# Attention steps over both key heads in halves of the TensorE array, with turning and values inside a later main tile

## What is computed

```python
s = jnp.einsum('bnqhgd,bnjhd->bnhgqj', qb, kb) * (HEAD_DIM ** -0.5)
s = jnp.where(valid, s, NEG_INF)
sk = sink.reshape(N_KV_HEADS, GQA_GROUP)
m = jnp.maximum(jnp.max(s, axis=-1, keepdims=True), sk)
e = jnp.exp(s - m)
p = e / (jnp.sum(e, axis=-1, keepdims=True) + jnp.exp(sk - m))
o = jnp.einsum('bnhgqj,bnjhd->bnqhgd', p, vb)
```

## Time and profile before

| | before |
|---|---|
| median of 3 runs | 1231.93 us |
| runs from, to | 1230.93, 1232.09 us |
| the profiled execution | 1237.62 us |
| its span | 1235.9 us |
| TensorE / VectorE / ScalarE / GpSimd busy | 97% / 56% / 30% / 6% |
| TensorE in the chain that ended last | 88% |

### The profile page before, as it was taken

How to read it: one execution, slowest core, us unless ns; L and a number is a source line. 1 busy time by engine, 2 the same in 40 slices (tenths; PEclk the granted TensorE clock), 3 DMA queues, 4 the chain that set the end, 5 groups by cost and what they waited for, 6 DMA issues and landing times.

```text
span 1235.9 us, 17238 instructions
## 1 busy us (share of the span) xinstructions
PE 1195.6 (97%) x6524; PEld 1090.1 (88%) x6524; DVE 691.9 (56%) x1146; ACT 365.1 (30%) x550; POOL 74.9 (6%) x104
## 2 busy tenths in 40 slices
PE   6979999999999999999999999999999999999997
PEld 1576668888899999999979999999999999999886
DVE  3777786887535575445645677653365333233434
ACT  3541114443451111232133532113311231123324
POOL 1100110000111111000000000000000000000000
PEclk7989999999999999999999999999999999999998
DMA  8833454231133232246421244332233221221212
GB/s 296 326 111 102 142 184 168 86 103 62 42 120 116 94 112 94 94 153 230 134 93 61 86 136 145 127 119 68 68 112 109 68 68 51 68 68 65 72 34 102
DMA packets 42528, 138.67 MB, mean 112 GB/s; under 512 B 4539, under 2 KB 10251, under 8 KB 41452
## 3 DMA queue, kind: packets, MB, share of 16 engines
q1 hardware_dynamic: 26832, 83.19, 20.0%
q0 software_dynamic: 10592, 41.95, 9.8%
q10 hardware_dynamic: 5052, 12.81, 3.0%
HBM read 122.20 MB, written 15.74 MB: 112 GB/s over the span
## 4 chain that ended last, share of the span: by engine, by line
PE 88%; DVE 7%; DMA 2%; issue 2%; ACT 1%; SPq 0%; DVEq 0%; ACTq 0%
PE acc_ps L561 61%; PE acc_ps L631 10%; PE wk L852 3%; PE wk L678 2%; PE wk L772 2%; PE wk L792 2%; PE wk L830 2%; DMA mod_raw<-in_w_ada_rows 1%; PE wk L782 1%; PE wk L671 1%; PE acc_ps L638 1%; DVE hy_cross L1605 1%; DVE dot_out L1404 1%; PE wk L592 1%; DMA hy_spec<-spec 1%
## 5 line engine op out<-in xcount | busy, mean ns | idle before, releaser
L561 PE MATMUL acc_ps<-act_hilo,w_hi 128*128 128x384 f32 x2304 | 510.2, 342 | 7.2 <-DVE act_hilo L1357 3.8
L561 PEld LDWEIGHTS acc_ps<-act_hilo,w_hi 128*128 128x128 f32 x2304 | 410.4, 189 | 29.1 <-issue 23.7
L561 PE MATMUL acc_ps<-act_hilo,w_lo 128*128 128x384 f32 x1152 | 294.2, 336 | 0.0
L1311 DVE TENSOR_TENSOR w_lo<-w_raw,w_hi 128x1024 fp32r<-128x1024 f32 x102 | 124.8, 1223 | 173.5 <-ACT w_hi L1001 172.5
L561 PEld LDWEIGHTS acc_ps<-act_hilo,w_lo 128*128 128x128 f32 x1152 | 209.8, 189 | 0.0
L1001 ACT ACTIVATE w_hi<-w_raw 128x1024 fp32r<-128x1024 f32 x102 | 108.0, 1059 | 286.8 <-PE acc_ps L561 283.2
L561 PE MATMUL acc_ps<-hidden_hilo,w_hi 128*128 128x384 f32 x768 | 164.0, 334 | 0.0
L561 PEld LDWEIGHTS acc_ps<-hidden_hilo,w_hi 128*128 128x128 f32 x768 | 135.9, 188 | 0.0
L561 PE MATMUL acc_ps<-hidden_hilo,w_lo 128*128 128x384 f32 x384 | 97.3, 334 | 0.0
L1715 DVE SCALAR_TENSOR_TENSOR xT<-acc_ps,modT,xT 128x384 f32 (+2 forms) x72 | 30.4, 479 | 89.8 <-PE acc_ps L561 89.3
L561 PEld LDWEIGHTS acc_ps<-hidden_hilo,w_lo 128*128 128x128 f32 x384 | 69.3, 188 | 0.0
(11 more groups left out here) (211 smaller groups left out, 1328.7 us busy)
## 6 DMA issues: line engine op xcount, KB each, us to landing
dot_ring<-in_w_ada_cols POOLq DMA_DIRECT2D x52, 512.0 KB, 3.7
w_raw<-in_w_pre SPq DMA_DIRECT2D x50, 512.0 KB, 3.4
w_raw<-in_w_up SPq DMA_DIRECT2D x32, 512.0 KB, 3.3
w_raw<-in_w_down SPq DMA_DIRECT2D x32, 512.0 KB, 3.3
mod_raw<-in_w_ada_rows SPq DMA_DIRECT2D x12, 512.0 KB, 8.1
spec<-filt_out POOLq DMA_DIRECT2D x12, 512.0 KB, 3.1
gate_spill<-gates_out ACTq DMA_DIRECT2D x16, 384.0 KB, 2.3
hy_spec<-spec SPq DMA_DIRECT2D x12, 512.0 KB, 5.7
```

The costliest lines, as they stand in the source:

```text
L561: mm = pe.matmul(acc_ps[:, slot, 512 * h:512 * h + HALF], w[:, kw, :], src[:, x, k, HALF * h:HALF * h + HALF], start=(first and i == 0), s ...
L1311: dve.tensor_tensor(lo, raw[s][:], hi, ALU.subtract).then_inc(lo_done, 1)
```

## The change

- A step is now a block of queries and a pair `jh` of query-head slots of *both* key heads: `scores` does its four matmuls in the order `ATT_ROWS` = 0, 2, 1, 3, so that the key head, and with it the row half, alternates. The sinks are laid out to match.
- `values` does two matmuls for each key block, one for each key head: 64 columns of `V` as stationary, the 256 columns of its two query heads as moving, into partitions 0-63 and 64-127 of one bank. `values_out` copies 128 partitions of 256 columns.
- `turned(n)` leaves the end of tile 8 + n and goes into tile 9 + n behind k-part 2, `values(n)` goes from behind k-part 1 to behind k-part 5 of the same tile. ScalarE copies `turned` just ahead of `values`, behind the exponentials.
- VectorE does `softmax_in` first in its turn of a tile, and `softmax_out` behind the dots; the 12 dots lie one in each of the tiles 6 to 17, not in 8 to 15.

```diff
-ATT = [(qb, kv) for qb in range(NTB) for kv in range(2)]
+ATT = [(qb, jh) for qb in range(NTB) for jh in range(2)]
+ATT_ROWS = (0, 2, 1, 3)
...
-for _n in range(len(ATT)):
-    STAGES[T_HY + 2 + _n].append(("turned", _n))
...
-for _n, _t in enumerate((8, 9, 10, 10, 11, 11, 12, 12, 13, 13, 14, 15)):
+for _n, _t in enumerate(range(T_HY, T_HY + 12)):
     DOTS_AT[_t].append(SDOT + 12 + _n)
...
             def scores(n):
 
-                qb, kv = ATT[n]
+                qb, jh = ATT[n]
                 first, nk, _ = att_keys(qb)
-                h = slice(HD * kv, HD * kv + HD)
-                for j in range(NJ):
-                    c = take("scores", n, j)
+                for i, r in enumerate(ATT_ROWS):
+                    kv, j = r // 2, 2 * jh + r % 2
+                    h = slice(HD * kv, HD * kv + HD)
+                    c = take("scores", n, i)
                     pe.matmul(wk[:, c:c + P * nk], qk[h, j, P * qb:P * qb + P], qk[h, 4, P * first:P * (first + nk)],
                               start=True, stop=True).then_inc(s_ready, 1)
...
                     pe.wait_ge(p_copied, done + kb + 1)
-                    mm = pe.matmul(wk[:, c:c + 512], V[:, first + kb, :], PT[:, n % 2, kb, :],
-                                   start=(kb == 0), stop=(kb == nk - 1))
+                    for kv in range(2):
+                        mm = pe.matmul(wk[HD * kv:HD * kv + HD, c:c + 256], V[:, first + kb, HD * kv:HD * kv + HD],
+                                       PT[:, n % 2, kb, 256 * kv:256 * kv + 256], start=(kb == 0), stop=(kb == nk - 1))
                 mm.then_inc(o_ready, 1)
...
                 def after(k):
-                    if k == 1:
+                    if k == 2:
+                        turned(VALUES_AT[t])
+                    if k == 5:
                         values(VALUES_AT[t])
                 return after
...
             def values_out(n):
-                qb, kv = ATT[n]
-                h = slice(HD * kv, HD * kv + HD)
+                qb, jh = ATT[n]
                 act_e.wait_ge(o_ready, n + 1)
                 c = bank("values", n, 0)
-                act_e.activation(qk[h, 0:NJ, P * qb:P * qb + P], wk[h, c:c + 512].rearrange("p (j n) -> p j n", j=NJ),
+                act_e.activation(qk[:, 2 * jh:2 * jh + 2, P * qb:P * qb + P], wk[:, c:c + 256].rearrange("p (j n) -> p j n", j=2),
                                  ACT.Copy).then_inc(o_copied, 1)
...
-                for kind, n in STAGES[t]:
-                    if kind == "turned":
-                        turned_out(n)
                 split_w(t + 2)
...
                 if t + 1 in VALUES_AT:
+                    turned_out(VALUES_AT[t + 1])
                     values_out(VALUES_AT[t + 1])
...
             for t in range(T_MERGE):
+                scored = [n for kind, n in STAGES[t] if kind == "scores"]
+                for n in scored:
+                    softmax_in(n)
                 if T_HY <= t < T_GATE:
                     conv_sides(t)
...
-                if "scores" not in [kind for kind, _ in STAGES[t]]:
-                    for d in DOTS_AT[t]:
-                        dot(d)
+                for d in DOTS_AT[t]:
+                    dot(d)
+                for n in scored:
+                    softmax_out(n)
```

More of the change, by code:

```diff
@@ L291, in program @@
             if t in VALUES_AT:
-                use("values", VALUES_AT[t], [(o_copied, VALUES_AT[t] + 1)])
+                n = VALUES_AT[t]
+                use("turned", n, [(p_copied, p_first[n] + kb + 1) for kb in range(att_keys(ATT[n][0])[1])])
+                use("values", n, [(o_copied, n + 1)])
             for kind, n in STAGES[t]:
@@ L295, in program @@
                     use(kind, n, [(s_max, NJ * n + j + 1) for j in range(NJ)])
-                elif kind == "turned":
-                    use(kind, n, [(p_copied, p_first[n] + kb + 1) for kb in range(att_keys(ATT[n][0])[1])])
                 elif kind == "turn":
@@ L854, in inverse @@
                         mm.then_inc(inv_ready, 1)
-            run = {"scores": scores, "turned": turned, "turn": turn, "forward": forward, "inverse": inverse}
+            run = {"scores": scores, "turn": turn, "forward": forward, "inverse": inverse}
             def between(t):
@@ L1170, in split_out @@
                 act_e.activation(act[:, 0, k, :], src, ACT.Copy).then_inc(sp_hi, 1)
-            run = {"scores": expo, "turned": lambda n: None, "turn": turn_out, "inverse": inverse_out,
+            run = {"scores": expo, "turn": turn_out, "inverse": inverse_out,
                    "forward": lambda n: None}
@@ L1568, in softmax_in @@
                     dve.wait_ge(p_ready, sum(att_keys(q)[1] for q, _ in ATT[:n - 1]))
-                for j in range(NJ):
-                    c = bank("scores", n, j)
-                    dve.wait_ge(s_ready, NJ * n + j + 1)
+                for i, j in enumerate(ATT_ROWS):
+                    c = bank("scores", n, i)
+                    dve.wait_ge(s_ready, NJ * n + i + 1)
                     dve.tensor_tensor_reduce(S[:, b, j, 0:P * nk], wk[:, c:c + P * nk], mask[:, m0:m0 + P * nk],
-                                             HD ** -0.5, sink[:, NJ * kv + j:NJ * kv + j + 1], ALU.add, ALU.max,
+                                             HD ** -0.5, sink[:, NJ * jh + j:NJ * jh + j + 1], ALU.add, ALU.max,
                                              mx[:, b, j:j + 1]).then_inc(s_max, 1)
@@ L1576, in softmax_in @@
                 dve.tensor_scalar(nmx[:, b], mx[:, b], -1.0, None, ALU.mult).then_inc(s_neg, 1)
-                dve.tensor_tensor(sd[:, b], sink[:, NJ * kv:NJ * kv + NJ], mx[:, b], ALU.subtract).then_inc(s_sd, 1)
+                dve.tensor_tensor(sd[:, b], sink[:, NJ * jh:NJ * jh + NJ], mx[:, b], ALU.subtract).then_inc(s_sd, 1)
             def softmax_out(n):
@@ L1639, in _ @@
             steps_y = [0]
-            def attend(n, t):
-                softmax_in(n)
-                for d in DOTS_AT[t]:
-                    dot(d)
-                softmax_out(n)
             def split_out(k):
@@ L1650, in split_out @@
                 dve.tensor_tensor(act[:, 1, k, :], src, act[:, 0, k, :], ALU.subtract).then_inc(sp_lo, 1)
-            run = {"turned": lambda n: None, "turn": turn_low, "forward": products,
-                   "inverse": combine}
+            run = {"turn": turn_low, "forward": products, "inverse": combine}
             for t in range(T_MERGE):
+                scored = [n for kind, n in STAGES[t] if kind == "scores"]
+                for n in scored:
+                    softmax_in(n)
                 if T_HY <= t < T_GATE:
@@ L1679, in _ @@
                     filt_out(f)
-                if "scores" not in [kind for kind, _ in STAGES[t]]:
-                    for d in DOTS_AT[t]:
-                        dot(d)
+                for d in DOTS_AT[t]:
+                    dot(d)
+                for n in scored:
+                    softmax_out(n)
                 for kind, n in STAGES[t]:
-                    if kind == "scores":
-                        attend(n, t)
-                    else:
+                    if kind != "scores":
                         run[kind](n)
@@ L1908, in laid_out @@
     h = {n: np.asarray(inputs[n]) for n in _RAW}
+    h["attn_sink"] = h["attn_sink"].reshape(2, 2, 2).transpose(1, 0, 2).reshape(h["attn_sink"].shape)
     x = np.concatenate([np.asarray(inputs["x_sample"])[0], np.asarray(inputs["x_prompt"])[0]], axis=0)
```

## The result

The changed kernel takes 1215.4 us, the median of 4 runs (1214.64 to 1220.31), beside 1231.43 us for the kernel before; the ratio is 0.9865 with a 95% interval from 0.9847 to 0.9883, so 1.35% less. The profiled execution took 1215.11 us (span 1213.3).

What follows compares the result with a forecast made beforehand. TensorE's instruction sum was taken to bound the kernel up to values(11), then the chain behind it. Scores -9.0, values -9.5, switches +4.2, waits -1.2, tail +4.0 gave -11.5 us: 1220.4 us, range 1216.5 to 1231 us.

Steps and rivals of the forecast that it cites:

- What bounds the kernel: First scores to first inverse transform: TensorE's sum counts up to values(11), then the distance from values(11) until 382.82 us.
- Scores: Scores steps on TensorE: alternating row halves end after 5 passes, not 8, saving 9.0 us.
- Values: Values steps on TensorE: column halves overlap to 2nk + 1 passes, saving 9.5 us, lower bound nothing.
- the extra 5.6 us: Scores and values: further gain from a fourth overlapped pass, part of it taken into the range's low end of 1216.5 us.
- Shape switches: Values inside the main tile: twelve round trips from the whole array at 0.35 us, +4.2 us (3.6 to 4.8).
- Waits that go: Values steps: waits on VectorE's maxima of the scores disappear with the new order, -1.2 us.
- VectorE's order: Maxima ahead of side terms and low weights, one dot per tile: VectorE stays under TensorE, 0 us.
- Turning, copies: Turning moved to k = 2 of the next tile, 0 us; copies for values hidden with about 1 us to spare.
- The tail: Tile 20 to the first inverse transform: values(11) comes 4.2 us later, copy some 0.2 us less, +4.0 us.
- B: Only one of scores' row halves and values' column halves overlaps: 1229.9 us rows only, 1229.4 us columns only; chance 0.15.
- C: Neither scores' nor values' halves overlap; switches, tail and waits leave +7.0 us, 1238.9 us; chance 0.16.
- A: Both scores' row halves and values' column halves overlap: 1220.4 us; chance 0.64.

Runs made afterwards that it cites:

- values split: Changed kernel with values' first key block behind k-part 5, the rest behind k-part 6; first scores to first inverse transform 181.4 us, against 174.6 us.
- places alone: Old scores and values steps at the changed kernel's places, with its VectorE order and spread dots; first scores to first inverse transform 194.9 us, 191.7 us before.
- values on the whole array: Changed kernel with values as one 512-column matmul per key block and two copies; first scores to first inverse transform 183.0 us, against 174.6 us.
- values in order A.. B..: Changed kernel with all key blocks of column half 0, then all of half 1; first scores to first inverse transform 177.7 us, against 174.6 us.

## Why the prediction was wrong, point by point

- **What bounds the kernel**: right. TensorE's sum counts up to values(11), the chain over the tables behind it; both regimes are in the chain of after.
- **Scores: the step that failed.** "I count this: A1, then A2 beside B1 ..., the last pass ends after 5 passes", and "If B1 could start with A1 it would be one pass more per step; ... I don't take it". The rows show program order only among matmuls that use the same part of the array. They could not speak on the order between halves, and I took them as if they did. In the kernel, two scores of different halves start together, and 4 passes are enough. The saving is 12.0 us (4 x 1.28 + 8 x 0.86) instead of 9.0 us.
- **Values: the same error.** 2nk passes, not 2nk + 1: 4 x 1.13 + 8 x 0.71 = 10.2 us from the rows, which already hold 0.15 us of each shape change. In passes alone it is 12.0 us (28 key blocks of two passes of 0.43 us, halved) instead of 9.5 us. Together the two are 3.0 + 2.6 = 5.6 us of passes, and the forecast missed the stretch by 5.5 us. With them the sum closes: -12.0 - 12.0 + 4.2 - 1.2 + 3.7 = -17.3 us, beside 17.0 us measured. The price was in the text as the bound of an unknown cost ("the extra 5.6 us"), and the low end of the range took only part of it.
- **Shape switches**: right, 0.35 to 0.4 us a round trip, 4.6 us in twelve against 4.2 us taken. The Trainium skill (TensorEngine Tiling (Array Packing), Key Properties) says that changing the tiling mode drains TensorE; the runs agree that every such change costs time, by that number, and no run here shows the drain itself.
- **Waits that go**: right. No wait of values on maxima is left in after. That it hangs on VectorE's order, which I booked at nothing, the experiment with the old order shows: 11.6 us if it is undone. The booking was right for the change, and silent on what the cover was worth.
- **Turning, copies**: right, nothing waits.
- **The tail**: right in size, partly by luck. The gap is 3.1 us (3.5 foreseen) and the forward transform 1.6 us slower. The inverse, which waited 1 us before, doesn't wait now: 3.1 + 1.6 - 1.0 = 3.7 us against 4.0. The forecast had 1.5 us of wait ahead of the inverse, on the products, and the lower clock hidden in it. Instead the first product stands 6.6 us behind the issue of the spectra load, not 7.75 us as before, so the products are ready early and all but 0.2 us of the clock's 1.6 us shows. Why the load is faster there stays open.
- **The rivals**: neither B nor C; A holds, with more overlap than it counted. Row halves and column halves both overlap fully, and the column halves' shared bank and partitions cost nothing. I trusted them less without a row that said so. The Trainium skill (TensorE: Matmul & The Clock Gate, Part 3) gives 2.38 times for three column tiles, which no run here tried. The estimate of 1.6 times for two that I had worked out from it was too low: from pass to pass two halves are 2.0 times one (0.32 us for two passes of 384 columns at once, 0.32 us for one before).

## What to carry to other kernels

Matmuls in different halves of the array start together if both have their operands, also where the program has another of the first half between them (two ahead cost nothing here, three cost 0.48 us), so count passes per half and not in program order; here a step in halves costs half of its passes and 0.35 to 0.4 us for leaving and re-entering the whole array. A faster step moves the deadlines of everything that frees its banks: reorder the engine that reads them first, or about half of the gain goes into waits (11.6 and 9.2 us here). And where the last step of a chain starts another chain, place it by hand, apart from the pattern of the others.

## What was unexpected in the hardware

- Two fp32 matmuls in the two row halves, or in the two column halves, begin within 0.02 us of each other and take the time of one: 4 matmuls of 384 columns in 1.49 us instead of 2.77, with 0.2 us for the shape in both.
- The other half's matmul overtakes one matmul that stands ahead of it and can't start yet. With three of the first half ahead of it, it waited until the first of them was through (1.93 instead of 1.45 us for values of three blocks). Whether the limit is a count of matmuls, of passes or of weight loads was not tried.
- A gap of 3.1 us in front of the forward transform made its 48 matmul records take 7.3 us once and again, and 5.8 us without one. Longer gaps didn't always cost more: 8.4 us behind a gap of 4.1 us (values split), but 7.3 us behind 3.5 and 3.7 us (places alone, values on the whole array), and 8.5 us behind 3.1 us (values in order A.. B..).
